# The down products of three MLP groups as seven products per quad of blocks and two token halves

## The chip, the cores and the metric

One core of a Trainium2 chip. The metric is the device time of one execution in microseconds; before the change three runs gave 1750.44, 1750.79 and 1751.02 us.

## The reference, cut to what matters

Two transformer blocks in float32 on x[1, 512, 1024]. The first has differential and forgetting attention with a gated MLP; the second, on the output of the first, has two layers (a short convolution, then latent attention), each with a squared-ReLU MLP. The change concerns the MLP of the last layer alone:

```python
def squared_relu_mlp(h, w_up, w_down):
    return jnp.square(jax.nn.relu(h @ w_up)) @ w_down      # 1024 -> 4096 -> 1024

    h = modulate(rmsnorm_2(x, norm_g[l, 2]), sh_f, sc_f)
    y = squared_relu_mlp(h, mlp_up_w[l], mlp_down_w[l])
    x = x + g_f[:, None, :] * rmsnorm_2(y, norm_g[l, 3])
```

## The kernel before, in words

Activations lie transposed: 128 features in the partitions, 512 tokens in the free dimension, so x, y and h are 8 tiles of 128x512. All weights come as one stream of blocks of 128x1024 (`wstream`); a block holds, for 128 output features, the 8 pieces of 128x128 for the 8 input tiles. Every operand of a matmul is split in a high part (rounded to the type fp32r) and a low part (the rest), and a product is three matmuls: high by high, high weight by low activation, low weight by high activation (L2032 to L2034). A block of 8 pieces is 24 matmuls of 512 columns into one PSUM bank.

A weight block passes four stations, each with 4 slots. SP loads it into `w_raw` (L739) as soon as the low part of the block four before is made (`wlo_done`); ScalarE makes the high part (`split_hi`, L815), three blocks ahead of TensorE (`AHEAD`); VectorE makes the low part (`split_lo`, L1206); TensorE uses both. A bank is reused four blocks later, when VectorE has evacuated it (`bank_free`).

`make_plan` (L76) writes the order of the stages, and each engine goes through this list on its own, in program order, with semaphores between them. At the start of each stage ScalarE and VectorE drain their pipelines (L1086, L1879). The last MLP has four groups of 1024 hidden features: an up stage (`relu2`, 8 blocks) writes 8 hidden tiles, a down stage (`acc`, 8 blocks) adds their products to y. Of each up block, ScalarE takes the ReLU out of PSUM (L893), VectorE multiplies it by the bank (L1433), ScalarE makes the high part (L895) and VectorE the low part (L1316, `rhs_ready`). In a down stage VectorE makes a low part, waits for the product and adds the bank to y (L1397 the first time, L1399 after). The last group ends with a tail of three blocks in two halves of 256 tokens (L2351 to L2353).

VectorE also works off 112 rows of a modulation product (`weighted`, L1217), whose rows POOL loads (L762); eight of them lie in the first down stage of the last MLP, one per block. An up stage without such rows is a loop on VectorE.

In the down stage VectorE's step, here without the cases of other stages, is:

```python
split_lo(t.n + AHEAD, (t.n0 + AHEAD) % SPLIT)
dve.wait_ge(out_done, t.o + 1)
dve.tensor_tensor(dst, dst, bank, ALU.add).then_inc(bank_free, 1)
```

## Time and profile before

| | |
|---|---|
| median of the runs | 1750.79 us (1750.44 to 1751.02) |
| span of the profiled execution | 1748.6 us, 2.2 us under the median of the runs |
| TensorE matmuls | 1730.2 us, 99% of the span, 8136 of them |
| VectorE, ScalarE, POOL | 1100.9, 628.6, 99.1 us |
| granted TensorE clock, mean | 0.999 of 2.4 GHz |
| weights | 283 blocks of 512 KB, 3.6 us each from issue to landing |

Busy time of matmuls overlaps: one of 512 columns is shown with 0.39 us, but the next starts 0.23 us later, so pace is read from starts. The idle time of an engine is shown ahead of the instruction that ended it, with what released it. The span runs from the first to the last instruction. The page gives no time of the profiled execution beyond this span.

### The profile page before, as it was taken

To read this page: it belongs to the slowest core of one execution; us is meant where nothing else is said; L and a number is where in the kernel's file an instruction comes from. 1 tells how busy PE (TensorE), PEld (TensorE's weight loads), DVE (VectorE), ACT (ScalarE), POOL (GpSimd) and SP (SyncE) were. 2 spreads that over 40 slices of the span, in tenths; PEclk is the share of its full clock that TensorE was granted. 3 is DMA by queue.
4 is the path that set the end of the run, shared out by engine and by line. 5 is a ranking of instruction groups with operands and counts; after the bars stand their busy time and mean duration, and the time that the engine had idled before them with its cause. 6 is when DMAs were issued, how large, how long until landed. Compare 5 with 4: busy or idle time off the path is not lost. (4 is left out here: it accounts for less than half of the span.)

```text
span 1748.6 us, 22691 instructions
## 1 busy us (share of the span) xinstructions
PE 1730.2 (99%) x8136; PEld 1404.5 (80%) x8136; DVE 1100.9 (63%) x1641; ACT 628.6 (36%) x991; POOL 99.1 (6%) x158
## 2 busy tenths in 40 slices
PE   9999999999999999999999999999999999999998
PEld 8777777888888888888888888887767888888887
DVE  7866555655555576878656565688775965434356
ACT  5236444322222353243423241444444442323241
POOL 0000000000000000100100101002000100000001
PEclk9999999999999999999999999999999999999999
DMA  7321112454444434652255555531411234323231
GB/s 248 110 96 37 49 49 76 153 169 147 147 162 153 136 102 135 219 184 94 84 180 191 194 192 193 180 109 54 121 61 49 85 101 164 104 88 107 86 97 48
DMA packets 62095, 216.63 MB, mean 124 GB/s; under 512 B 7232, under 2 KB 9408, under 8 KB 61824
## 3 DMA queue, kind: packets, MB, share of 16 engines
q1 hardware_dynamic: 45072, 154.95, 26.2%
q0 software_dynamic: 16656, 60.04, 11.1%
q8 instruction: 49, 0.80, 0.2%
q10 hardware_dynamic: 288, 0.59, 0.1%
q14 instruction: 30, 0.25, 0.0%
HBM read 212.67 MB, written 2.10 MB: 123 GB/s over the span
## 5 line engine op out<-in xcount | busy, mean ns | idle before, releaser
L815 ACT ACTIVATE w_hi<-w_raw 128x1024 fp32r<-128x1024 f32 x283 | 297.7, 1053 | 378.3 <-PE psum L2034 338.9
L1206 DVE TENSOR_TENSOR w_lo<-w_raw,w_hi 128x1024 fp32r<-128x1024 f32 x283 | 346.1, 1223 | 118.6 <-ACT w_hi L815 109.7
L2032 PE MATMUL psum<-h_hi,w_hi 128*128 128x512 f32 x1056 | 411.7, 390 | 0.0
L2033 PE MATMUL psum<-h_lo,w_hi 128*128 128x512 f32 x1056 | 410.8, 389 | 0.0
L2034 PE MATMUL psum<-h_hi,w_lo 128*128 128x512 f32 x1056 | 410.8, 389 | 0.0
L2032 PE MATMUL psum<-hid_hi,w_hi 128*128 128x512 f32 x728 | 283.2, 389 | 0.0
L2033 PE MATMUL psum<-hid_lo,w_hi 128*128 128x512 f32 x728 | 283.2, 389 | 0.0
L2034 PE MATMUL psum<-hid_hi,w_lo 128*128 128x512 f32 x728 | 283.2, 389 | 0.0
L2032 PEld LDWEIGHTS psum<-h_hi,w_hi 128*128 128x128 f32 x1056 | 198.2, 188 | 41.7 <-issue 0.5
L2033 PEld LDWEIGHTS psum<-h_lo,w_hi 128*128 128x128 f32 x1056 | 198.2, 188 | 41.6 <-issue 0.5
L2034 PEld LDWEIGHTS psum<-h_hi,w_lo 128*128 128x128 f32 x1056 | 198.2, 188 | 41.4
L2034 PEld LDWEIGHTS psum<-hid_hi,w_lo 128*128 128x128 f32 x728 | 136.6, 188 | 28.5
L2033 PEld LDWEIGHTS psum<-hid_lo,w_hi 128*128 128x128 f32 x728 | 136.6, 188 | 28.4
L2032 PEld LDWEIGHTS psum<-hid_hi,w_hi 128*128 128x128 f32 x728 | 136.6, 188 | 28.2
L1217 DVE SCALAR_TENSOR_TENSOR ada_raw<-ada_raw,c_row 128x1024 f32<-128x1024 f32 x112 | 136.4, 1219 | 0.9 <-DMA ada_raw<-in_ada 0.8
L762 POOL DMA_DIRECT2D ada_raw<-in_ada x112 | 59.3, 530 | 1134.0 <-DVE ada_raw L1217 1092.1
L1316 DVE TENSOR_TENSOR hid_lo<-scratch,hid_hi 128x512 fp32r<-128x512 f32 (+1 forms) x94 | 65.1, 693 | 75.7 <-ACT hid_hi L895 52.7
L1433 DVE TENSOR_TENSOR scratch<-scratch,psum 128x512 f32<-128x512 f32 x64 | 43.9, 686 | 90.0 <-ACT scratch L893 90.0
L893 ACT ACTIVATE scratch<-psum 128x512 f32<-128x512 f32 x64 | 38.1, 596 | 141.5 <-PE psum L2034 134.6
L1399 DVE TENSOR_TENSOR y<-y,psum 128x512 f32<-128x512 f32 (+1 forms) x37 | 25.4, 688 | 89.7 <-PE psum L2034 89.6
L2007 PE MATMUL psum<-h_hi,w_hi 128*128 128x512 f32 x152 | 61.3, 403 | 1.6 <-ACT h_hi L1113 1.0
L895 ACT ACTIVATE hid_hi<-scratch 128x512 f32 (+1 forms) x64 | 40.5, 633 | 60.2 <-DVE scratch L1433 60.2
(346 smaller groups left out, 2003.6 us busy)
## 6 DMA issues: line engine op xcount, KB each, us to landing
w_raw<-in_wstream SPq DMA_DIRECT2D x283, 512.0 KB, 3.6
ada_raw<-in_ada POOLq DMA_DIRECT2D x112, 512.0 KB, 3.8
x<-in_xT SPq DMA_DIRECT2D x8, 256.0 KB, 5.7
outT<-x SPq DMA_DIRECT2D x16, 128.0 KB, 1.8
con<-in_consts SPq DMA_DIRECT2D x1, 1032.0 KB, 10.0
w_raw<-in_wstream SPq DMA_DIRECT2D x4, 256.0 KB, 4.9
con<-in_rope ACTq DMA_DIRECT2D x1, 576.0 KB, 6.5
c_row<-in_crow POOLq DMA_DIRECT2D x1, 512.0 KB, 4.1
```

Of the source, the lines that this page charges most:

```text
L762: pool.dma_start(ada_raw[:, half, :], ada[v]).then_inc(ada_loaded[half], 16)
L815: act.activation(w_hi[:, slot, :], w_raw[:, slot, :], ACT.Copy).then_inc(whi_done, 1)
L893: act.activation(scratch[:, 2 + t.j % 2, :], bank, ACT.Relu).then_inc(gate_done, 1)
L895: act.activation(tile_of(hi_out, t.b), scratch[:, 8, :], ACT.Copy).then_inc(hi_done, 1)
L1206: dve.tensor_tensor(w_lo[:, slot, :], w_raw[:, slot, :], w_hi[:, slot, :].bitcast(F32), ALU.subtract).then_inc(wlo_done, 1)
L1217: dve.scalar_tensor_tensor(out=row, in0=row, scalar=1.0, in1=c_row[:, :], op0=ALU.mult, op1=ALU.mult, accum_out=ada_sum[:, u:u + 1]).then_ ...
L1316: dve.tensor_tensor(tile_of(lo_out, d), scratch[:, 8, :], tile_of(hi_out, d).bitcast(F32), ALU.subtract).then_inc(rhs_ready, 1)
L1433: dve.tensor_tensor(val, scratch[:, 2 + t.j % 2, :], bank, ALU.mult).then_inc(bank_free, 1)
L2007: pe.matmul(bank, w_hi[:, slot, w], hi[:, ra + k, :], start=k == 0, stop=False)
L2032: pe.matmul(bank, w_hi[:, slot, w], hi[:, ra + k, :], start=k == 0, stop=False)
L2033: pe.matmul(bank, w_hi[:, slot, w], lo[:, ra + k, :], start=False, stop=False)
L2034: mm = pe.matmul(bank, w_lo[:, slot, w], hi[:, ra + k, :], start=False, stop=k == nk - 1)
```

## The change

In the first three groups of the last MLP the down stage (8 blocks) becomes a stage `quads` of two quads. A quad is four blocks: two by two pieces of the weight, where the output side is split in two pairs of 128 features and the input side in even and odd hidden tiles. The tokens are split in two halves of 256, so the activations are two by two pieces as well. The product of these two-by-two matrices is made from seven products instead of eight, by sums of weights, sums of activations and sums of results. Each of the seven, named A12, A11, A, B, C, D, A22 in this order, has 2 output blocks x 4 input pieces x 3 = 24 matmuls of 256 columns and fills one bank.

- Weights. A = a21 + a22 is made by transfers: SP loads a21 into the slot, then POOL issues a transfer of a22 that adds to it. B = A + A11 and C = B + A12 are made by VectorE in slots of `w_raw`, D = A11 + a21 by VectorE in a buffer `w_diff`, into which SP loads a21 once more. Blocks of a quad: four before, six transfers now.
- Activations. In the up stages of these groups the hidden tiles are taken in pairs. After each second tile VectorE makes four sums of 256 columns (`pair_sums`), ScalarE copies three high parts (the odd tile, the even tile, the three sums as one of 768 columns) and VectorE makes the three low parts.
- Results. B accumulates in the bank of A11, C in that of A, D in that of B; each waits for the evacuation before it. VectorE evacuates each product into y, D into two places.
- VectorE's order in step t of `quads`: the weight sums due up to four products ahead, the low part of product t + 3, then the evacuation of product t. In the first step B and C are due, in the second D.
- The first quad of a stage does the first three input pieces of A12 and A11, then the last one of both.
- The eight modulation rows go from the first down stage to the up stage of the last group. SP's loop over blocks is written out, the ring of POOL's descriptors is set to 8192 bytes, and the tail's root takes another bank.

```diff
+    def quads(hid, first):
+        add("quads", dict(n=QUADS * QUAD, o=QUADS * QUAD, quad=QUADS), r0=hid, first=first)
+    def mlp(h, up, down, *names, ends=0, paired=(), **last):
         for g in range(4):
             hid = counts["rhs"]
-            gemm("relu2", 8, "h", h, kouter=AHEAD if g == 0 else 0, presplit=1 if g == 0 else 0, rows=up[g])
+            gemm("relu2", 8, "h", h, kouter=AHEAD if g == 0 else 0, presplit=1 if g == 0 else 0, rows=up[g],
+                 paired=g in paired)
             if g == 3:
                 take(*names)
+            if g in paired:
+                quads(hid, g == 0)
+                continue
             gemm("acc", 8 - (ends if g == 3 else 0), "hid", hid, dst="y", first=g == 0, sq=g == 3, rows=down[g],
                  go_on=ends > 0, **(last if g == 3 else {}))
...
-    hid = mlp(h, (0, 0, 0, 0), (8, 0, 0, 0), "r_f1", ends=ENDS)
+    hid = mlp(h, (0, 0, 0, 8), (0, 0, 0, 0), "r_f1", ends=ENDS, paired=(0, 1, 2))
...
+                a12, a11, a21, a22 = range(at_block, at_block + 4)
+                for u, src in ((U_A12, (a12,)), (U_A11, (a11,)), (U_A, (a21, a22)), (U_B, ()), (U_C, ()), (U_D, (a11, a21)),
+                               (U_A22, (a22,))):
...
+        def quad_bank(s, u):
+            return psum[:, (s["at"]["o"] + QUADS * QUAD + (0, 2, 1, 2, 1, 2, 3)[u]) % BANKS, :]
+        def quad_operand(u, k):
+            if u == U_A11 or u == U_A:
+                col = slice(0, HALF) if u == U_A11 else slice(HALF, S)
+                return hid_hi[:, 2 * k, col], hid_lo[:, 2 * k, col]
+            if u == U_A12 or u == U_C:
+                col = slice(0, HALF) if u == U_A12 else slice(HALF, S)
+                return hid_hi[:, 2 * k + 1, col], hid_lo[:, 2 * k + 1, col]
+            g = {U_B: 1, U_D: 0, U_A22: 2}[u]
+            return sums_hi[:, g, k, :], sums_lo[:, g, k, :]
...
+            for n in range(RAW, NB):
+                u, src, quad = SOURCE[n]
+                slot = n % RAW
+                if u in (U_B, U_C, U_D):
+                    continue
                 sp.wait_ge(wlo_done, n + 1 - RAW)
-                src = wstream[n] if isinstance(n, int) else wstream[bass.ds(n, 1)].rearrange("a p m -> (a p) m")
-                sp.dma_start(w_raw[:, slot, :], src).then_inc(raw_loaded[slot], 16)
-
-            with sp.Fori(1, NB // RAW) as i:
-                for j in range(RAW):
-                    load(RAW * i + j, j)
-            for n in range(NB // RAW * RAW, NB):
-                load(n, n % RAW)
+                made = 2 * sum(SOURCE[m][0] == U_C for m in range(n)) - (1 if SOURCE[n - 1][0] == U_C else 0)
+                if made and (u == U_A22 or any(SOURCE[m][0] is not None for m in range(n - RAW, n))):
+                    sp.wait_ge(sum_made, 2 * quad + 1 if u == U_A22 else 2 * quad if u is not None else made)
+                if u == U_A:
+                    sp.dma_start(w_raw[:, slot, :], wstream[src[0]]).then_inc(sum_begun, 16)
+                    if quad:
+                        sp.wait_ge(wlo_done, last_of(U_D, n) + 1)
+                    sp.dma_start(w_diff[:, :], wstream[SOURCE[n - U_A + U_D][1][1]]).then_inc(diff_loaded, 16)
+                else:
+                    sp.dma_start(w_raw[:, slot, :], wstream[src[0]]).then_inc(raw_loaded[slot], 16)
...
+                if s["kind"] == "quads":
+                    for q in range(QUADS):
+                        n, k = s["at"]["n"] + q * QUAD, s["at"]["quad"] + q
+                        slot = (n + U_A) % RAW
+                        pool.wait_ge(sum_begun, 16 * (k + 1))
+                        pool.dma_start(w_raw[:, slot, :], wstream[SOURCE[n + U_A][1][1]], accum_op=ALU.add)\
+                            .then_inc(sum_loaded, 16)
+                        pool.wait_ge(sum_loaded, 16 * (k + 1))
+                        pool.sem_inc(raw_loaded[slot], 16)
...
+                        if s.get("paired"):
+                            if t.b % 2:
+                                i, p = t.b // 2, at_["pair"] + t.b // 2
+                                act.wait_ge(bank_free, BANKS + t.o + 1)
+                                act.activation(hid_hi[:, t.b, :], scratch[:, 1, :], ACT.Copy).then_inc(hi_done, 1)
+                                act.wait_ge(pair_step, 4 * p + 2)
+                                act.activation(hid_hi[:, t.b - 1, :], scratch[:, 0, :], ACT.Copy).then_inc(hi_done, 1)
+                                act.wait_ge(pair_step, 4 * p + 4)
+                                act.activation(sums_hi[:, :, i, :], pair_sum[:, :, :], ACT.Copy).then_inc(hi_done, 1)
...
+                for t in range(QUADS * QUAD):
+                    n = n0 + t + AHEAD
+                    u, _, quad = SOURCE[n]
+                    if u == U_D:
+                        act.wait_ge(out_done, o0 + t)
+                        act.wait_ge(diff_made, quad + 1)
+                        act.activation(w_hi[:, n % SPLIT, :], w_diff[:, :], ACT.Copy).then_inc(whi_done, 1)
+                    else:
+                        split_hi(n // RAW + 1, n % SPLIT, o0 + t)
...
+            def pair_sums(p):
+                b11, b12, b21, b22 = (scratch[:, i, half_of(h)] for i in range(2) for h in range(2))
+                g3, g2, g4 = (pair_sum[:, i, :] for i in range(3))
+                dve.tensor_tensor(g3, b22, b12, ALU.subtract).then_inc(pair_step, 1)
+                dve.wait_ge(pair_step, 4 * p + 1)
+                dve.tensor_tensor(b12, b11, b12, ALU.subtract).then_inc(pair_step, 1)
+                dve.wait_ge(pair_step, 4 * p + 2)
+                dve.scalar_tensor_tensor(out=g2, in0=b22, scalar=-1.0, in1=b12, op0=ALU.mult, op1=ALU.subtract).then_inc(pair_step, 1)
+                dve.wait_ge(pair_step, 4 * p + 3)
+                dve.scalar_tensor_tensor(out=g4, in0=g2, scalar=-1.0, in1=b21, op0=ALU.mult, op1=ALU.subtract).then_inc(pair_step, 1)
+            def quads(s):
+                n0, o0 = s["at"]["n"], s["at"]["o"]
+                def weight_sum(n):
+                    u, _, quad = SOURCE[n]
+                    if u == U_D:
+                        m = n - U_D + U_A11
+                        dve.wait_ge(diff_loaded, 16 * (quad + 1))
+                        dve.wait_ge(raw_loaded[m % RAW], 16 * (m // RAW + 1))
+                        dve.tensor_tensor(w_diff[:, :], w_raw[:, m % RAW, :], w_diff[:, :], ALU.add).then_inc(diff_made, 1)
+                        return
+                    slot, before = n % RAW, (n - 1) % RAW
+                    other = (n - 2) % RAW if u == U_B else slot
+                    for m in (n - 1, n - 2 if u == U_B else n - 4):
+                        dve.wait_ge(raw_loaded[m % RAW], 16 * (m // RAW + 1))
+                    dve.wait_ge(wlo_done, n - RAW + 1)
+                    dve.tensor_tensor(w_raw[:, slot, :], w_raw[:, before, :], w_raw[:, other, :], ALU.add)\
+                       .then_inc(raw_loaded[slot], 16)
+                    dve.wait_ge(raw_loaded[slot], 16 * (n // RAW + 1))
+                    dve.sem_inc(sum_made, 1)
+                def of_tiles(Q, i, h):
+                    return y[:, 4 * Q + i:4 * Q + i + 3:2, half_of(h)]
+                sums = [n0 + Q * QUAD + u for Q in range(QUADS) for u in (U_B, U_C, U_D)]
+                for t in range(QUADS * QUAD):
+                    Q, u = divmod(t, QUAD)
+                    n, o = n0 + t, o0 + t
+                    while sums and sums[0] <= n + AHEAD + 1:
+                        weight_sum(sums.pop(0))
+                    m = n + AHEAD
+                    if SOURCE[m][0] == U_D:
+                        dve.wait_ge(whi_done, m + 1)
+                        dve.tensor_tensor(w_lo[:, m % SPLIT, :], w_diff[:, :], w_hi[:, m % SPLIT, :].bitcast(F32),
+                                          ALU.subtract).then_inc(wlo_done, 1)
+                        dve.sem_inc(raw_loaded[m % RAW], 16)
+                    else:
+                        split_lo(m, m % SPLIT)
+                    bank = quad_bank(s, u).rearrange("p (a n) -> p a n", a=2)
+                    dve.wait_ge(out_done, o + 1)
+                    dve.wait_ge(bank_free, BANKS + o)
+                    into = {U_A12: (0, 0), U_A11: (0, 0), U_A: (1, 1), U_B: (0, 1), U_C: (0, 1), U_D: (1, 0), U_A22: (1, 0)}[u]
+                    dst = of_tiles(Q, *into)
+                    fresh = s["first"] and u in (U_A12, U_A, U_B, U_D)
+                    minus = u in (U_A, U_D, U_A22)
+                    if u == U_D:
+                        also = of_tiles(Q, 1, 1)
+                        dve.tensor_tensor(also, also, bank, ALU.subtract)
+                    if fresh and minus:
+                        z = dve.tensor_scalar(dst, bank, -1.0, None, ALU.mult)
+                    elif fresh:
+                        z = dve.tensor_copy(dst, bank)
+                    else:
+                        z = dve.tensor_tensor(dst, dst, bank, ALU.subtract if minus else ALU.add)
+                    z.then_inc(bank_free, 1)
...
+                        i, odd = divmod(t.b, 2)
+                        dve.wait_ge(gate_done, at_["gate"] + t.b + 1)
+                        dve.wait_ge(rhs_ready, at_["rhs"] + 3 * i)
+                        dve.tensor_tensor(scratch[:, odd, :], scratch[:, 2 + t.j % 2, :], bank, ALU.mult).then_inc(bank_free, 1)
+                        if odd:
+                            dve.wait_ge(bank_free, BANKS + t.o + 1)
+                            pair_sums(at_["pair"] + i)
+                            for part, (lo, val, hi) in enumerate((
+                                    (hid_lo[:, t.b, :], scratch[:, 1, :], hid_hi[:, t.b, :]),
+                                    (hid_lo[:, t.b - 1, :], scratch[:, 0, :], hid_hi[:, t.b - 1, :]),
+                                    (sums_lo[:, :, i, :], pair_sum[:, :, :], sums_hi[:, :, i, :]))):
+                                dve.wait_ge(hi_done, at_["hi"] + 3 * i + part + 1)
+                                dve.tensor_tensor(lo, val, hi.bitcast(F32), ALU.subtract).then_inc(rhs_ready, 1)
...
+                def product(Q, u, ks):
+                    n = n0 + Q * QUAD + u
+                    bank = quad_bank(s, u)
+                    adds = u in (U_B, U_C, U_D)
+                    for part in range(2):
+                        out = bank[:, half_of(part)]
+                        for k in ks:
+                            hi, lo = quad_operand(u, k)
+                            w = slice((4 * part + k) * P, (4 * part + k + 1) * P)
+                            pe.matmul(out, w_hi[:, n % SPLIT, w], hi, start=not adds and part == 0 and k == 0, stop=False,
+                                      skip_group_check=True)
+                            pe.matmul(out, w_hi[:, n % SPLIT, w], lo, start=False, stop=False, skip_group_check=True)
+                            mm = pe.matmul(out, w_lo[:, n % SPLIT, w], hi, start=False, stop=True, skip_group_check=True)
+                    return mm
+                for Q in range(QUADS):
+                    n, o = n0 + Q * QUAD, o0 + Q * QUAD
+                    free = (o - 2, o - 4, o - 1, o + U_A11, o + U_A, o + U_B, o - 3) if Q == 0 else \
+                        (o - QUAD + U_A12, o - QUAD + U_D, o - QUAD + U_C, o + U_A11, o + U_A, o + U_B, o - QUAD + U_A22)
+                    if Q == 0:
+                        for ks in (range(3), range(3, 4)):
+                            for u in (U_A12, U_A11):
+                                if ks[0] == 0:
+                                    pe.wait_ge(wlo_done, n + u + 1)
+                                    pe.wait_ge(bank_free, BANKS + free[u] + 1)
+                                pe.wait_ge(rhs_ready, s["r0"] + 3 * ks[-1] + (1 if u == U_A12 else 2))
+                                mm = product(Q, u, ks)
+                                if ks[0] == 3:
+                                    mm.then_inc(out_done, 1)
+                        pe.wait_ge(rhs_ready, s["r0"] + 3 * 4)
+                    for u in range(2 if Q == 0 else 0, QUAD):
+                        pe.wait_ge(wlo_done, n + u + 1)
+                        pe.wait_ge(bank_free, BANKS + free[u] + 1)
+                        product(Q, u, range(4)).then_inc(out_done, 1)
...
+    nc = bacc.Bacc("TRN2", target_bir_lowering=False, num_devices=1, dynamic_dma_scratch_size=8192)
```

## Rows read from the trace of the kernel before

**Rows 1.** The page, part 1: busy us, share of the span, instructions of each engine.
```profile
PE 1730.2 (99%) x8136; PEld 1404.5 (80%) x8136; DVE 1100.9 (63%) x1641; ACT 628.6 (36%) x991; POOL 99.1 (6%) x158
```
**Rows 2.** TensorE's waits, longest first: waiter, releaser, us in total, times, longest.
```profile
PE psum L1995 <- DVE eps L1196: 1.6, 1, 1.6
```
**Rows 3.** Windows, first and third down stage: length, busy us, granted clock, DMA share, GB/s.
```profile
1432.46:1475.98 43.52, 43.52 (x193) 36.04 (x192) 23.41 (x31) 9.72 (x10) 3.23 (x6) 1.00 0.49 173
...
1606.54:1650.06 43.52, 43.52 (x193) 36.04 (x192) 16.01 (x17) 9.73 (x10) 0.00 (x0) 1.00 0.36 107
```
**Rows 4.** Timeline of TensorE, tail's second half: start, us, line, operands, count.
```profile
1731.96 0.29 PE L2353 MATMUL psum<-hid_hi,w_lo 128*128 128x256 f32 x1
...
1738.80 0.28 PE L2353 MATMUL psum<-hid_hi,w_lo 128*128 128x256 f32 x1
```
**Rows 5.** Timeline of TensorE, first matmul of the first down stage.
```profile
1432.46 0.39 PE L2032 MATMUL psum<-hid_hi,w_hi 128*128 128x512 f32 x1
```
**Rows 6.** Timeline of VectorE, first down stage and the up stage behind it.
```profile
1433.29 0.69 DVE L1433 TENSOR_TENSOR scratch<-scratch,psum 128x512 f32<-128x512 f32 x1 [1.88 <-ACT scratch L893]
1434.68 0.69 DVE L1316 TENSOR_TENSOR hid_lo<-scratch,hid_hi 128x512 fp32r<-128x512 f32 x1 [0.70 <-ACT hid_hi L895]
...
1438.10 0.69 DVE L1397 COPY y<-psum 128x512 f32<-128x512 f32 x1 [0.72 <-PE psum L2034]
1438.71 1.22 DVE L1217 SCALAR_TENSOR_TENSOR ada_raw<-ada_raw,c_row 128x1024 f32<-128x1024 f32 x1
...
1439.85 1.22 DVE L1206 TENSOR_TENSOR w_lo<-w_raw,w_hi 128x1024 fp32r<-128x1024 f32 x1
...
1478.34 1.23 DVE L1206 TENSOR_TENSOR w_lo<-w_raw,w_hi 128x1024 fp32r<-128x1024 f32 x1 [0.33 <-DVEq L1879]
1482.42 0.69 DVE L1433 TENSOR_TENSOR scratch<-scratch,psum 128x512 f32<-128x512 f32 x1 [2.85 <-ACT scratch L893]
```
**Rows 7.** Timeline of VectorE in the tail: operations of 256 columns.
```profile
1733.97 0.48 DVE L1610 SCALAR_TENSOR_TENSOR psum<-y,r_f,psum 128x256 f32<-128x256 f32 x1
1734.49 0.42 DVE L1625 TENSOR_TENSOR x<-x,psum 128x256 f32<-128x256 f32 x1
1734.83 0.47 DVE L1610 SCALAR_TENSOR_TENSOR y<-y,r_f,psum 128x256 f32<-128x256 f32 x1
```
**Rows 8.** Groups of ScalarE, 1340 to 1749 us: line, operands, count, busy, mean ns, idle before.
```profile
L815 ACT ACTIVATE w_hi<-w_raw 128x1024 fp32r<-128x1024 f32 x69 | 72.7, 1053 | 115.5 <-PE psum L2034 114.5 <-ACTq L1086 1.0
...
L895 ACT ACTIVATE hid_hi<-scratch 128x512 f32 x24 | 15.2, 633 | 21.0 <-DVE scratch L1433 21.0
```
**Rows 9.** Timeline of TensorE, its last matmuls.
```profile
1740.09 0.70 PE L2337 MATMUL psum<-scratch,mean 128*128 128x256 f32 x2 [0.58 <-ACT scratch L1076]
```
**Rows 10.** Windows behind the last matmul, columns as in rows 3.
```profile
1743.00:1744.00 1.00, 0.00 (x0) 0.00 (x0) 1.00 (x4) 0.00 (x0) 1.00 (x2) 0.84 0.14 48
1744.00:1748.60 4.60, 0.00 (x0) 0.00 (x0) 2.07 (x6) 0.00 (x0) 1.02 (x2) 0.50 0.66 218
```
**Rows 11.** Windows of line L1995 (128x128 matmuls) at the opening: length, busy, clock, DMA.
```profile
1.56:6.30 4.74, 4.74 (x22) 1.00 0.97 249
6.30:6.95 0.65, 0.65 (x8) 1.00 1.03 359
```
**Rows 12.** The page, part 6: transfers, count, KB each, median us to landing.
```profile
w_raw<-in_wstream SPq DMA_DIRECT2D x283, 512.0 KB, 3.6
ada_raw<-in_ada POOLq DMA_DIRECT2D x112, 512.0 KB, 3.8
...
con<-in_consts SPq DMA_DIRECT2D x1, 1032.0 KB, 10.0
```
**Rows 13.** Window of the opening, columns as in rows 3.
```profile
10.00:20.00 10.00, 10.00 (x45) 8.16 (x44) 9.16 (x13) 9.23 (x15) 0.00 (x0) 1.00 1.04 413
```
**Rows 14.** The page, part 5: the loads issued by POOL.
```profile
L762 POOL DMA_DIRECT2D ada_raw<-in_ada x112 | 59.3, 530 | 1134.0 <-DVE ada_raw L1217 1092.1
```

More of the change, by code:

```diff
@@ L52 @@
 ROOT_WARM, NEW_WARM = 3, 7
+QUAD, QUADS = 7, 2
+U_A12, U_A11, U_A, U_B, U_C, U_D, U_A22 = range(QUAD)
 SHIFT = 1
@@ L78, in make_plan @@
     counts = dict(n=0, o=0, gate=0, tap=0, sqv=0, ss=0, val=0, hi=0, rhs=0, xup=0, sqa=0, aux=0, rstd=0,
-                  take=0, gains=4, ada=0, rope=0, xpool=0, vs=0, step=0, shift=0)
+                  take=0, gains=4, ada=0, rope=0, xpool=0, vs=0, step=0, shift=0, pair=0, quad=0)
     plan = []
@@ L103, in gemm @@
         if evac == "relu2":
-            inc.update(gate=nblk, hi=nblk, rhs=nblk)
+            parts = nblk // 2 * 3 if about.get("paired") else nblk
+            inc.update(gate=nblk, hi=parts, rhs=parts, pair=nblk // 2 if about.get("paired") else 0)
         if evac == "conv":
@@ L291, with weight_sources @@
 NB = TOTALS["n"]
+def weight_sources():
+    table, at_block = {}, 0
+    for s, after in zip(PLAN, [p["at"]["n"] for p in PLAN[1:]] + [NB]):
+        n = s["at"]["n"]
+        if s["kind"] == "quads":
[3 more added lines that the diff above has]
+                               (U_A22, (a22,))):
+                    table[n + u] = (u, src, s["at"]["quad"] + q)
+                n += QUAD
+                at_block += 4
+        while n < after:
+            table[n] = (None, (at_block,), None)
+            n += 1
+            at_block += 1
+    return table, at_block
+SOURCE, BLOCKS = weight_sources()
 LAST_GEMM = max(i for i, s in enumerate(PLAN) if s["kind"] == "gemm")
@@ L776, in _ @@
                     done = upto
+                if s["kind"] == "quads":
+                    for q in range(QUADS):
+                        n, k = s["at"]["n"] + q * QUAD, s["at"]["quad"] + q
[5 more added lines that the diff above has]
+                        pool.sem_inc(raw_loaded[slot], 16)
                 if s["kind"] == "renew":
@@ L902, in step @@
                         act.activation(tile_of(hi_out, t.of(3) + s.get("f0", 0)), scratch[:, 8, :], ACT.Copy).then_inc(hi_done, 1)
-                steps(act, s, step, last)
+                if s.get("paired"):
+                    for b in range(s["nblk"]):
+                        step(Step(s, b, b, 0, s["nblk"]))
+                else:
+                    steps(act, s, step, last)
+            def quads(s):
[9 more added lines that the diff above has]
+                        split_hi(n // RAW + 1, n % SPLIT, o0 + t)
             def open_stage(s):
@@ L2493, in tiles, with push_quads @@
         return w.reshape(K // P, P, M // P, P).transpose(2, 1, 0, 3).reshape(M // P, P, K)
+    def push_quads(w):
+        t = tiles(w).reshape(2, 2, 2, P, DT // 2, 2, P)
+        t = t.transpose(0, 2, 5, 3, 1, 4, 6).reshape(2, 4, P, D)
+        blocks.append(t[:, (1, 0, 2, 3)].reshape(8, P, D))
     def push(t, per=1):
@@ L2519, in lay_out, with mlp @@
     push(tiles(f["conv_out_w_2"][0]))
-    def mlp(l):
+    def mlp(l, paired=()):
         for g in range(4):
             push(tiles(f["mlp_up_w_2"][l][:, g * D:(g + 1) * D]))
-            push(tiles(f["mlp_down_w_2"][l][g * D:(g + 1) * D]))
+            down = f["mlp_down_w_2"][l][g * D:(g + 1) * D]
+            push_quads(down) if g in paired else push(tiles(down))
     mlp(0)
```

41 lines of the change are left out of this document (32 added, 9 removed).

## Prediction

> **What bounds the kernel now.** I read the page's busy shares first: TensorE is busy for 1730.2 of 1748.6 us, VectorE for 63% and ScalarE for 36% [rows 1]. Then TensorE's waits: the longest is 1.6 us, and that is the opening [rows 2]. So the time is TensorE's, and only fewer TensorE cycles, or a new hole in its stream, can change it. Third, the stretches of the last MLP: a down group takes 43.52 us with TensorE busy for all of it at full granted clock, while VectorE is busy for 16 to 23 us [rows 3].
>
> Times are worked out against the profiled execution, whose span is 1748.6 us; the median of the runs, 1750.79 us, is 2.2 us more. That remainder lies at start and end, which the change leaves alone, so I add differences to the median.
>
> **TensorE's work.** A down group is 8 blocks of 24 matmuls of 512 columns, one every 0.2267 us (43.52 / 192) [rows 3]. The 256-column form exists in the tail: from 1731.96 to 1738.80 us there are 57 steps, 0.120 us each [rows 4]. Half the columns therefore cost 53% of the time. A quad goes from 4 x 24 x 0.2267 = 21.76 us to 7 x 24 x 0.120 = 20.16 us, a group of two quads from 43.52 to 40.32 us. Gain: 3.20 us a group, 9.6 us in all, where seven eighths of the time would have been 16.3 us.
>
> **VectorE at the handover, the first quad of each group.** Let 0 be the start of a group's first matmul (1432.46 in the trace [rows 5]). Unit prices on VectorE: a 1024-column operation lasts 1.22 us and lets the next start after 1.14; a 512-column one 0.69 and 0.61 [rows 6]. In the tail a 256-column scalar_tensor_tensor lasts 0.48, a tensor_tensor 0.42, and one that needs the result of the one before starts 0.04 after its end [rows 7].
>
> Before, the last square is multiplied on VectorE from 0.83 to 1.52 and its low part is done at 2.91 [rows 6]; TensorE has seven earlier tiles to work on meanwhile, so nothing waits. Now the chain goes on: four dependent operations of pair_sums (2 x 0.46 + 2 x 0.52) from 1.56 to about 3.46. Low parts of two tiles, paced by 0.61, end at about 4.1 and 4.7. The high part of the three sums (768 columns) starts on ScalarE when pair_sums ends; between 0.63 for 512 and 1.05 for 1024 columns [rows 8] I take 0.84, so 4.35. Its low part starts at 4.6 and lasts between 0.69 and 1.22, say 0.96: 5.55. The stage's fence on VectorE costs 0.33 [rows 6]: 5.9.
>
> Then the quads stage, in program order: weight sum B (1.22 + 0.04 for the wait on itself + 0.05 for the semaphore step, 1.3), weight sum C (1.3), low part of B (1.14), evacuation of A12 (0.61), weight sum D (1.14), low part of C (1.14), evacuation of A11 (0.69). Together 7.3: the bank of A11 is free at 13.2, known to TensorE at 13.3.
>
> TensorE meanwhile: the first two products in portions, 36 + 12 matmuls of 0.12, to 5.76 (their waits at 4.1 and 4.7 are just met), product A to 8.64. Product B accumulates into the bank of A11, so it waits for that evacuation: **a hole of 4.65 us in every group**. From there both engines run in step. A quad asks VectorE for ten 1024-column operations and eight of 512, 10 x 1.14 + 8 x 0.61 = 16.3 of 20.16 us, so it keeps up, and so does ScalarE with 7 x 1.05 = 7.4 us.
>
> A group becomes 40.32 + 4.65 = 44.97 us instead of 43.52, 1.45 us more, 4.35 us for three. Bounds of the hole: if every wait and latency on VectorE were free and only its pacing counted (0.83 + 0.61 + 2 x 0.34 + 2 x 0.39 + 2 x 0.61 + 0.87 + 5 x 1.14 + 0.61 + 0.69), A11 would be free at 12.0 and the hole 3.3, hardly more than the gain. If a semaphore step costs 0.2 and the 768-column operations as much as 1024-column ones, it is 5.4, which makes 2.2 us a group. I take 4.65, since nearly each duration in it has a row.
>
> **TensorE's clock after the hole.** After its last matmul, which ends at 1740.79 [rows 9], TensorE stays idle; the granted clock is 0.84 in 1743 to 1744 us, and 0.50, the 1.2 GHz level, from 1744 on [rows 10]. A mean of 0.84 puts the fall at 1743.68, 2.9 us after that end. My hole is idle for 4.5 us (A's last matmul ends at 8.80), so the clock can fall in it. The price: at the opening the first 22 small matmuls take 4.74 us, 0.22 each, and the next 8 take 0.65, 0.08 each [rows 11] (the granted clock stands as 1.00 there, but the pace is that of a lower level). So some 4.7 us of work may pass before the full pace is back, at about half, and one fall costs about 2.4 us. With one delay seen, and a hole only 1.6 us longer, I count one fall in three holes: 2.4 us. Bounds: none (0) and all three (7.1).
>
> **The accumulating transfer.** The trace has none. For the first quad of a group its slot is free four blocks ahead, over 20 us, so any price is hidden. For the second quad, the slot of A follows that of D, whose low part is done at 13.2 + 1.2 = 14.4. The load takes 3.6 us [rows 12]: 18.0. Then the accumulating one. VectorE comes to weight sum B of that quad at 23.4 (after product D's two evacuations), and needs 9.1 us from there to the evacuation of the second A11 at 32.5, which TensorE wants at 33.5. So the transfer, with POOL's waits, is hidden up to about 6.0 us, and each us more costs 1 us per group. From below, a plain 512 KB load by POOL lands in 3.8 us, and adding to what is there can't be quicker; from above, 1032 KB land in 10.0 in the crowded opening [rows 12]. I take 3.8 and a second pass over 512 KB at the 413 GB/s that the opening sustains [rows 13], 1.3: 5.1 us, hidden with under 1 us to spare. The rate is no matter: six transfers a quad are 156 GB/s.
>
> **The rest, at nothing.** The eight modulation rows (1.22 us each [rows 6]) go from the first down group to the last up group, where VectorE idles 2.85 us before a square [rows 6]; without that cover they would cost up to 9.8 us. In the up groups pair_sums and the low part of the sums add 2.9 us per two blocks (10.88 us), in the same idle time. SP's loads are written out instead of looped; its new waits are met by VectorE's weight sums, behind them stand loads alone, and the first that matters is priced above. POOL waits in its quads entries with nothing else due. The smaller descriptor area could only delay POOL's modulation loads, ahead of which POOL sat waiting for VectorE 1092.1 us in all [rows 14]. The tail's other bank changes no count.
>
> Sum: 1750.8 - 9.6 + 13.95 + 2.4 = **1757.5 us**.
>
> **Rivals.**
> - *The clock falls in every hole.* The idle time that the fall took at the end, 2.9 us, is shorter than each hole, and then each costs its 2.4 us: 1750.8 - 9.6 + 13.95 + 7.1 = 1762.2. Against: one fall seen, in an end where TensorE had stood for 0.58 us just before [rows 9], and no such hole in mid-kernel. 15%. The Trainium skill ("TensorE: Matmul & The Clock Gate", section "Why this matters for your kernels") speaks for it: it advises to leave no idle gaps between bursts of matmuls, because one is enough to bring the half clock back.
> - *The accumulating transfer is late.* Its time decides from 6.0 us on. At 8 us each second quad has a hole of 2 us more: 1757.5 + 6 = 1763.5; at 10 us, 1769.5. For it: the 10.0 of the large load, and that the load to w_diff is issued at the same moment. Against: the 3.8 of POOL's plain loads beside SP's. 18%.
> - *The hole is near its floor and the clock holds.* With holes of 3.3 to 4.3 us and no fall the sum is 1750.8 - 9.6 + 9.9 to 12.9 = 1751.1 to 1754.1. For it: the full clock in the rest of the stretch [rows 3]. Against: it needs VectorE's waits to vanish. 17%.
> - *The other side: the hole does not outgrow the gain.* VectorE gets to the evacuation of A11 early. It decides where that evacuation ends before 8.64 + 3.20 = 11.84, 1.4 us earlier than I find. With one weight sum and one low part less ahead of it, it ends at 10.8, the holes are 2.2 us, and the time is 1750.8 - 9.6 + 6.6 = 1747.8; with no hole it is 1741.2. For it: VectorE is idle for 20 to 27 of 43.5 us in a down group [rows 3]. Against: that idle time lies behind the handover, and the pacing alone gives 12.0. 8%.
> - *The forecast*: holes of about 4.65 us, a fall in some, the transfer hidden: 42%, by itself 1754.5 to 1760.
>
> Differences under 0.2% (3.5 us) cannot be told from none. Slower: 42 + 15 + 18 = 75%; within: 17%; faster: 8%. The range leaves out the faster case and the far end of the late transfer: 1752 to 1768.
>
> **What would show it.** In the profile after: 256-column matmuls of the quads in steps of 0.12 us; an idle stretch of TensorE of 4 to 5 us in each of the three groups, ahead of product B of the first quad, released by VectorE's evacuation; before that release two weight sums, a low part, an evacuation, a weight sum and a low part on VectorE without a break; and a dip of the granted clock where a hole was. A second hole, in the second quad and with POOL's transfer behind it, would show the late transfer. If no hole stands at product B, or the steps are over 0.13 us, the prediction is wrong in its main step.

## The result, and the profile after

| | before | after |
|---|---|---|
| median of the runs, us | 1750.9 (4 runs, 1750.44 to 1751.82) | 1762.8 (4 runs, 1761.47 to 1764.21) |
| profiled execution: span, us | 1748.6 | 1759.6 |
| TensorE busy, us | 1730.2 | 1726.7 |
| VectorE busy, us | 1100.9 | 1183.6 |

The ratio of the times is 1.0067 [1.0053, 1.0081]: slower, by 0.7%. The predicted 1757.5 us is 5.3 us too low, inside the range of 1752 to 1768.

The page's first part, after, answers to [rows 1]: TensorE works 3.5 us less and the program lasts 11.0 us more.
```profile
PE 1726.7 (98%) x8568; PEld 1422.6 (81%) x8568; DVE 1183.6 (67%) x1761; ACT 657.3 (37%) x1021; POOL 104.2 (6%) x164
```
Windows of the three changed down groups, after, columns as in [rows 3] (stretch, length, busy us of PE, PEld, DVE, ACT and POOL, granted clock, DMA share, GB/s):
```profile
1432.81:1479.82 47.01, 42.25 (x337) 41.90 (x336) 37.59 (x43) 17.43 (x18) 0.88 (x1) 0.96 0.50 144
1523.37:1570.95 47.58, 42.87 (x338) 42.69 (x337) 37.66 (x43) 17.43 (x18) 0.86 (x1) 0.93 0.51 144
1614.49:1661.04 46.55, 41.83 (x338) 41.65 (x336) 37.58 (x43) 17.43 (x18) 0.86 (x1) 0.96 0.51 147
sum 141.14, PE 126.95 PEld 126.24 DVE 112.84 ACT 52.29 POOL 2.59; mean PE 42.32 PEld 42.08 DVE 37.61 ACT 17.43 POOL 0.86
```
This is the whole account. Three groups took 3 x 43.52 = 130.56 us before and take 141.14 now: 10.6 of the span's 11.0 us. In them TensorE is idle for 141.14 - 126.95 = 14.2 us, and busy for 6.0 us more than the 3 x 40.32 that the shorter products need at full pace. So: 130.56 - 9.6 + 14.2 + 6.0 = 141.2. Not all of the 6.0 us is the clock: by the starts, the matmuls of the 6 us behind the three stops take 1.56, 2.39 and 1.35 us more than at 0.12 each, 5.3 in sum; most of the rest is the last matmul before each stop, which shows its whole 0.28 us because no next one overlaps it.

Where it is idle: TensorE's timeline in the first group, after (start, us, line, operands, count, in brackets the idle time before it and what ended it). Product A ends in steps of 0.12 us; product B starts 4.72 us later, released by VectorE's evacuation at L1481, and soon goes on in steps of 0.21 us, until 0.12 is back at 1450.04.
```profile
1441.20 0.28 PE L2294 MATMUL psum<-hid_lo,w_hi 128*128 128x256 f32 x1
1441.32 0.28 PE L2295 MATMUL psum<-hid_hi,w_lo 128*128 128x256 f32 x1
1446.32 0.36 PE L2292 MATMUL psum<-sums_hi,w_hi 128*128 128x256 f32 x1 [4.72 <-DVE y L1481]
1446.51 0.33 PE L2294 MATMUL psum<-sums_lo,w_hi 128*128 128x256 f32 x1
...
1449.42 0.41 PE L2292 MATMUL psum<-sums_hi,w_hi 128*128 128x256 f32 x1
1449.63 0.41 PE L2294 MATMUL psum<-sums_lo,w_hi 128*128 128x256 f32 x1
...
1450.04 0.28 PE L2292 MATMUL psum<-sums_hi,w_hi 128*128 128x256 f32 x1
1450.16 0.29 PE L2294 MATMUL psum<-sums_lo,w_hi 128*128 128x256 f32 x1
```
The same stop stands in the other two groups (4.71 and 4.72 us). Windows of the three stops and of what follows each, after, columns as above: the granted clock falls to 0.5, the 1.2 GHz level, at each of them, and comes back to 1.00 after 3 to 5 us of work. Over the stops themselves it is 1.00, 0.84 and 0.95 in the mean: at the first stop it fell only when work had begun again, at the others inside the stop.
```profile
1441.60:1446.32 4.72, 0.00 (x1) 0.03 (x1) 4.72 (x6) 2.67 (x3) 0.00 (x0) 1.00 0.54 199
1446.32:1450.00 3.68, 3.68 (x18) 3.68 (x19) 2.72 (x3) 0.22 (x1) 0.00 (x0) 0.54 0.70 188
1450.00:1452.00 2.00, 2.00 (x19) 2.00 (x18) 0.69 (x1) 1.04 (x1) 0.00 (x0) 1.00 0.91 287
1532.16:1536.87 4.71, 0.00 (x0) 0.03 (x1) 4.71 (x6) 2.66 (x3) 0.00 (x0) 0.84 0.62 202
1536.87:1542.00 5.13, 5.13 (x24) 5.13 (x25) 2.72 (x3) 0.22 (x1) 0.00 (x0) 0.50 0.69 241
1542.00:1544.00 2.00, 2.00 (x18) 2.00 (x18) 1.24 (x2) 1.06 (x1) 0.00 (x0) 0.96 0.43 168
1623.28:1628.00 4.72, 0.01 (x1) 0.03 (x1) 4.72 (x6) 2.67 (x3) 0.00 (x0) 0.95 0.58 193
1628.00:1631.00 3.00, 3.00 (x14) 3.00 (x15) 2.73 (x3) 0.22 (x1) 0.00 (x0) 0.51 0.73 191
1631.00:1633.00 2.00, 2.00 (x19) 2.00 (x19) 0.56 (x1) 0.56 (x1) 0.00 (x0) 1.00 0.90 281
```
What VectorE does meanwhile: its timeline from the last square of the up stage (answers to the first lines of [rows 6]) to the evacuation that TensorE waits for. From the first of these lines on, no bracket names TensorE; the chain is VectorE's own, without a break of over 0.33 us.
```profile
1433.64 0.69 DVE L1618 TENSOR_TENSOR scratch<-scratch,psum 128x512 f32<-128x512 f32 x1 [3.26 <-ACT scratch L977]
1434.36 0.43 DVE L1418 TENSOR_TENSOR pair_sum<-scratch 128x256 f32<-128x256 f32 x1
...
1436.08 1.29 DVE L1627 TENSOR_TENSOR hid_lo<-scratch,hid_hi 128x512 fp32r<-128x512 f32 x2
1437.29 0.95 DVE L1627 TENSOR_TENSOR sums_lo<-pair_sum,sums_hi 128x768 fp32r<-128x768 f32 x1
1438.57 1.23 DVE L1443 TENSOR_TENSOR w_raw<-w_raw 128x1024 f32<-128x1024 f32 x1 [0.33 <-DVEq L2077]
1440.11 1.23 DVE L1443 TENSOR_TENSOR w_raw<-w_raw 128x1024 f32<-128x1024 f32 x1 [0.31 <-DVE w_raw L1443]
1441.48 1.23 DVE L1318 TENSOR_TENSOR w_lo<-w_raw,w_hi 128x1024 fp32r<-128x1024 f32 x1
1442.62 0.68 DVE L1479 COPY y<-psum 128x512 f32<-128x512 f32 x1
1443.22 1.22 DVE L1436 TENSOR_TENSOR w_diff<-w_raw,w_diff 128x1024 f32<-128x1024 f32 x1
1444.35 1.22 DVE L1318 TENSOR_TENSOR w_lo<-w_raw,w_hi 128x1024 fp32r<-128x1024 f32 x1
1445.49 0.68 DVE L1481 TENSOR_TENSOR y<-y,psum 128x512 f32<-128x512 f32 x1
```
The accumulating transfer shows no stop of its own after (the longest step before product B of a second quad is 0.32 us in the first group). Its chain in the first group: D's low part ends at 1447.31 (14.5 us after the group's start), SP loads A's first term for the second quad (issued at 1447.33), POOL can issue the accumulating transfer only at 1453.00, and VectorE's weight sum B of that quad starts at 1458.93, after an idle time that no compute engine ended. Timelines of SP, POOL and VectorE, after:
```profile
1447.33 0.33 SPq L815 DMA_DIRECT2D w_raw<-in_wstream  x1
1447.71 0.42 SPq L818 DMA_DIRECT2D w_diff<-in_wstream  x1
...
1453.00 0.88 POOL L857 DMA_DIRECT2D w_raw<-in_wstream  x1 [31.36 <-DMA w_raw<-in_wstream]
...
1458.93 1.23 DVE L1443 TENSOR_TENSOR w_raw<-w_raw 128x1024 f32<-128x1024 f32 x1 [0.92 <-issue]
```
So load and accumulation take 5.7 + 5.9 us here, 6.3 + 5.5 and 5.3 + 5.8 in the other groups, where the prediction had 3.6 + 5.1. Experiments e6 to e8 ask why that cost nothing.

### The profile page after: what moved, and what is told of

It is laid out like the page before. It is cut to its first block and busy times, and to the rows that moved or that the text cites. A ratio compares the mean times of both kernels' runs of the same rounds, so it can differ in the third digit from the quotient of the medians.

```text
span 1759.6 us, 22662 instructions
## 1 busy us (share of the span) xinstructions
PE 1726.7 (98%) x8568; PEld 1422.6 (81%) x8568; DVE 1183.6 (67%) x1761; ACT 657.3 (37%) x1021; POOL 104.2 (6%) x164
## 5 line engine op out<-in xcount | busy, mean ns | idle before, releaser
L2234 PE MATMUL psum<-h_hi,w_lo 128*128 128x512 f32 x1056 | 410.8, 389 | 0.0
L2232 PE MATMUL psum<-hid_hi,w_hi 128*128 128x512 f32 x536 | 208.5, 389 | 0.0
L2233 PE MATMUL psum<-hid_lo,w_hi 128*128 128x512 f32 x536 | 208.5, 389 | 0.0
L2234 PE MATMUL psum<-hid_hi,w_lo 128*128 128x512 f32 x536 | 208.5, 389 | 0.0
L2234 PEld LDWEIGHTS psum<-hid_hi,w_lo 128*128 128x128 f32 x536 | 100.6, 188 | 21.0
L2233 PEld LDWEIGHTS psum<-hid_lo,w_hi 128*128 128x128 f32 x536 | 100.6, 188 | 20.9
L2232 PEld LDWEIGHTS psum<-hid_hi,w_hi 128*128 128x128 f32 x536 | 100.6, 188 | 20.8
L1500 DVE TENSOR_TENSOR hid_lo<-scratch,hid_hi 128x512 fp32r<-128x512 f32 x70 | 48.5, 692 | 54.2 <-ACT hid_hi L989 31.2
L2208 PE MATMUL psum<-h_hi,w_lo 128*128 128x512 f32 x152 | 59.4, 391 | 0.0
L1631 DVE TENSOR_TENSOR scratch<-scratch,psum 128x512 f32<-128x512 f32 x40 | 27.5, 687 | 46.6 <-ACT scratch L977 46.6
L2292 PE MATMUL psum<-sums_hi,w_hi 128*128 128x256 f32 x144 | 43.5, 302 | 14.2 <-DVE y L1481 14.2
```

The costliest lines, as they stand in the source:

```text
L1500: dve.tensor_tensor(tile_of(lo_out, d), scratch[:, 8, :], tile_of(hi_out, d).bitcast(F32), ALU.subtract).then_inc(rhs_ready, 1)
L2208: pe.matmul(bank, w_lo[:, slot, w], hi[:, ra + k, :], start=False, stop=False)
L2232: pe.matmul(bank, w_hi[:, slot, w], hi[:, ra + k, :], start=k == 0, stop=False)
L2233: pe.matmul(bank, w_hi[:, slot, w], lo[:, ra + k, :], start=False, stop=False)
L2234: mm = pe.matmul(bank, w_lo[:, slot, w], hi[:, ra + k, :], start=False, stop=k == nk - 1)
L2292: pe.matmul(out, w_hi[:, n % SPLIT, w], hi, start=not adds and part == 0 and k == 0, stop=False, skip_group_check=True)
```

## The experiments

The theory: the stop is VectorE's chain at the handover; the half clock behind it is a price on top; the transfer hides. The rivals: the chain is not what product B waits for, or the clock's price is no price.

**e1_warm_hole.** Keep TensorE at work in the stop, so that the clock can't fall:
```diff
                     for u in range(2 if Q == 0 else 0, QUAD):
+                        if Q == 0 and u == U_B:
+                            keep_warm(34)
                         pe.wait_ge(wlo_done, n + u + 1)
```


> The changed kernel with 34 small matmuls (128x128, into a bank that nobody reads) ahead of product B of each stage's first quad, about 4.2 us of work in a hole of 4.9 us. VectorE's chain is untouched, so product B still starts as late. Theory (hole plus clock): the granted clock holds, the 5.1 us that the three falls cost come back, and the time is 1757 us (1755.5 to 1758.5). Rival (the clock costs nothing of its own, the rest is lost elsewhere, as to the late transfer or to contention): it stays at 1762.8. Rival (the gate falls for another reason than idleness, such as the 256-column form): the dips stay and so does the time.

Measured: 1763.77 us (1763.37 to 1764.07), ratio 1.0076 [1.0062, 1.009]. The clock stayed at full, but I had mis-sized the filler: each of the 34 calls is two matmuls, so it lasts 7.76 us and outlives the stop by some 3 us. TensorE's timeline of e1:
```profile
1440.82 7.76 PE L2195 MATMUL psum<-mean 128*128 128x128 f32 x68
1448.34 0.36 PE L2292 MATMUL psum<-sums_hi,w_hi 128*128 128x256 f32 x1
```
The groups are 47.90 us long, 40.32 + 7.58. This run says nothing of the clock's price; e6 repeats it at the right size. It does answer the rival on the 256-column form: the same matmuls stand here, and with TensorE kept at work the clock did not fall.

**e2_sums_early.** Take the three weight sums of each group's first quad out of the handover, into the up stage's loop, where VectorE waits for squares:
```diff
+                        if s.get("paired"):
+                            for u in {4: (U_D,), 6: (U_B, U_C)}.get(b, ()):
+                                weight_sum(at_["n"] + s["nblk"] + u)
...
-                sums = [n0 + Q * QUAD + u for Q in range(QUADS) for u in (U_B, U_C, U_D)]
+                sums = [n0 + QUAD + u for u in (U_B, U_C, U_D)]
```


> The changed kernel with the three weight sums of each stage's first quad made by VectorE in the up stage (D after its fifth block, B and C after its seventh); the order within the quads stage stays. Theory: 3.7 us of weight sums leave the chain ahead of the evacuation of A11, the hole shrinks from 4.9 to about 0.8 us, too short for the clock to fall, and a group takes 41.3 us: 1750.9 + 0.4 - 6.7 = 1744.6 us (1743 to 1747), faster than before. Rival (the transfers are what costs): the weight sums were not the bound, the time stays above 1757. Rival (VectorE's work in the up stage now delays the hidden tiles): a hole appears at the start of the stage, and the time is 1748 or more.

Measured: 1750.26 us (1748.88 to 1755.25), ratio 1.0003 [0.9994, 1.0012]. The stop before product B of the first quad shrank as expected, in groups 2 and 3 from 5.00 to 0.82 us between starts: the chain is its cause. But 5.7 us of the expected gain are missing, because a stop opened elsewhere: before product B of the *second* quad, 3.02, 1.64 and 2.19 us between starts in the three groups, the first with a fall of the clock. Timelines of POOL, VectorE and TensorE in e2's second group:
```profile
1538.90 0.86 POOL L857 DMA_DIRECT2D w_raw<-in_wstream  x1 [34.46 <-DMA w_raw<-in_wstream]
...
1544.40 1.23 DVE L1440 TENSOR_TENSOR w_raw<-w_raw 128x1024 f32<-128x1024 f32 x1 [2.24 <-issue]
...
1553.71 0.35 PE L2295 MATMUL psum<-sums_hi,w_hi 128*128 128x256 f32 x1 [1.36 <-DVE y L1481]
```
VectorE is now idle for 2.24 us ahead of weight sum B, and starts 5.5 us after POOL's issue, which points to the transfer; e3 tests it. In group 1 the last of the expected rivals, late hidden tiles, came true as well: VectorE, with the early sums ahead of it, starts the last square 2.12 us after the group's start (0.83 in group 2), and TensorE stops for 1.11 us between starts at the first portions and for 0.99 before product B.

**e4_evac_first.** The changed kernel with one reorder: the first two evacuations of a quads stage ahead of its weight sums and low parts.
```diff
+                def low(t):
...
+                def evacuate(t):
...
+                evacuate(0)
+                evacuate(1)
+                for t in range(QUADS * QUAD):
+                    low(t)
+                    if t >= 2:
+                        evacuate(t)
```


> The changed kernel with nothing made earlier, only reordered: at the start of a quads stage VectorE evacuates A12 and A11 before it makes the weight sums. Theory: product B no longer waits for its bank but for its own weights (weight sums B, C and the low part of B lie ahead), the hole is split: 2.5 us before B, 1.2 before C, and about 1.3 in the second quad, as VectorE has no slack left. Each piece is shorter than the 2.9 us after which the clock fell in the idle end, so it holds: 1756.5 us (1754 to 1759). If the clock falls in pieces of 2.5 us too: 1760 or more. Rival (only the evacuation was the cause, the sums are free): no hole, 1742.

Measured: 1762.2 us (1760.55 to 1766.44), ratio 1.0073 [1.0059, 1.0087]. The stop went to 2.73 us between starts, near the 2.5 expected, and product B now waits for its own low part instead of the bank:
```profile
1443.94 0.39 PE L2302 MATMUL psum<-sums_hi,w_hi 128*128 128x256 f32 x1 [2.46 <-DVE w_lo L1318]
...
1468.66 0.55 PE L2302 MATMUL psum<-sums_hi,w_hi 128*128 128x256 f32 x1 [2.82 <-DVE y L1484]
```
What it saved came back twice: the clock fell at these stops as well, as the second expectation (1760 or more) had it, and second-quad stops of 3.10, 1.37 and 2.52 us opened (the second line above). The three groups together are 141.47 us, against 141.14.

**e5_all_early.** e2, e4's reorder, and SP's load of the second quad's A moved ahead (the diff of that move stands under e3).


> Weight sums of the first quad made in the up stage, evacuations of A12 and A11 first, and SP loads the second quad's A as soon as the sums of the first have read the slot, ahead of the three loads that stood before it. Theory: no hole is left in either quad, every group takes 40.3 us at the full clock: 1750.9 + 0.4 - 9.6 = 1741.7 us (1740.5 to 1744). Rival (a second limit in the quads stage, VectorE's share of 16.3 in 20.16 us or the transfer): holes appear elsewhere, and the time is 1746 or more.

Measured: 1741.73 us (1741.28 to 1742.93), ratio 0.9951 [0.9937, 0.9965], against the kernel before: faster than both. Windows of the three groups in e5:
```profile
1432.65:1473.61 40.96, 40.62 (x337) 40.41 (x336) 35.47 (x42) 17.32 (x18) 0.88 (x1) 1.00 0.54 166
1517.16:1557.47 40.31, 40.31 (x337) 40.31 (x336) 34.31 (x41) 17.32 (x18) 0.86 (x1) 1.00 0.56 159
1601.02:1641.33 40.31, 40.31 (x337) 40.31 (x336) 34.33 (x41) 17.32 (x18) 0.86 (x1) 1.00 0.53 160
```
Two groups run at 40.31 us without a stop; the prediction's price for TensorE's work was 40.32. The first has one step of 0.62 us at its first portions.

**e3_transfer_early.** e2 and SP's move alone, to test what the second-quad stops are:
```diff
+                if SOURCE[n][0] == U_A and SOURCE[n][2] % QUADS:
+                    order.remove(n)
+                    order.insert(order.index(n - QUAD + U_A22 - U_A), n)
...
+                if u == U_A and quad % QUADS:
+                    sp.wait_ge(wlo_done, n - QUAD + U_A11 - U_A + 1)
+                    sp.wait_ge(sum_made, 2 * quad - 1)
+                    sp.wait_ge(diff_made, quad)
+                    sp.dma_start(w_raw[:, slot, :], wstream[src[0]]).then_inc(sum_begun, 16)
+                    continue
```


> The three weight sums of each group's first quad made in the stage before, as in e2, and besides SP loads the first term of the second quad's A as soon as the low part of the first quad's A11 is made, instead of behind D's low part. Nothing else moves. Theory (in e2 the second-quad stops of 3.0, 1.6 and 2.2 us are the transfer: sum B of the second quad waits for it, 5.9 us of load and 5.5 us of accumulation after D's low part): these stops and the clock dip in group 1 go, the 0.83 us stop before product B of the first quad stays, groups of about 41.0 us, 1744 us. Rival (the second-quad stops come from VectorE's own backlog, which the early sums only moved): the stops stay, 1750 us.

Measured: 1744.77 us (1743.86 to 1747.12), ratio 0.9968 [0.9956, 0.998]. The second-quad stops are gone from all three groups, the 0.83 us stop stays in groups 2 and 3. So they were the transfer, load and accumulation together, and not VectorE's backlog. Group 1 keeps stops of 1.16 us at its first portions and 1.00 before product B, as in e2.

**e6_warm_20, e7_early_only, e8_warm_early.** If the transfer is that late, why has the changed kernel no stop at it? Either it had time enough there, or the stretch at half clock made TensorE late as well. Two edits, each alone and both together: e1's filler with 20 calls instead of 34, and SP's early load.

> As e1, dummy matmuls of 128 columns on TensorE in the stop before product B of the first quad, but 20 calls (40 matmuls of 0.114 us, 4.56 us) instead of 34 (7.76 us, which was longer than the stop), so that product B starts where it did. Their result is used nowhere. Clock theory (the price of the falls, 1.5 + 2.3 + 1.3 = 5.1 us, is all on the path): groups of 45.2 us, 1757.7 us. Rival (two covers: in the changed kernel the second quad's transfer is ready, and with it the evacuation of the second A11, only 35.3, 35.5 and 34.8 us after the group's start, where a TensorE without clock falls would come at 33.7): the clock holds, but a stop of 1.1 to 1.9 us opens before product B of the second quad in each group, groups of 46.4 to 47.1 us, about 1762 us.

> The changed kernel with one move alone: SP loads the first term of the second quad's A early, as in e3. Both theories: the stop before product B of the first quad stays at 4.7 us and the clock falls in it, so the transfer's lateness stays covered by the half-clock stretch: 1762.4 us, within 1 us of the changed kernel. A third one, that the transfer itself holds VectorE or TensorE up through traffic: 1758 or less.

> e6 and e7 together: the 20 dummy calls in the stop, and the early load for the second quad's A. Clock theory: as e6 alone, 1757.7 us, so no difference between e6 and e8. Two covers: only now both are gone, each group is 40.32 + 4.9 = 45.2 us, 1757.5 us, about 4.5 us less than e6 and 5 us less than e7.

| second-quad load | clock falls in the stop | clock kept up |
|---|---|---|
| late, as in the change | 1762.8 (the changed kernel) | e6: 1759.64 (1758.94 to 1761.26) |
| early | e7: 1762.65 (1760.41 to 1764.04) | e8: 1757.35 (1756.62 to 1757.47) |

The ratios to the kernel before are 1.0054 [1.004, 1.0068] for e6, 1.0066 [1.0053, 1.008] for e7 and 1.0038 [1.0025, 1.0052] for e8. With the falls in place the early load gains nothing; with the clock kept up it gains 2.3 us. With the early load the clock is worth 5.3 us; without it, 3.1 (2.3 by the ratios, since the changed kernel's own runs stand beside others of the kernel before; the intervals of these two ratios overlap). The sums of the three groups in the profiled executions agree in the order: 141.14 us for the changed kernel, and, columns as above, the first group and the sum of e6 and e7:
```profile
1432.23:1478.47 46.24, 45.23 (x377) 44.90 (x376) 37.59 (x43) 17.43 (x18) 0.88 (x1) 1.00 0.50 148
sum 139.92, PE 135.71 PEld 134.70 DVE 112.72 ACT 52.09 POOL 2.59; mean PE 45.24 PEld 44.90 DVE 37.57 ACT 17.36 POOL 0.86
...
1434.49:1481.89 47.40, 42.68 (x338) 42.50 (x336) 37.67 (x43) 17.54 (x18) 0.88 (x1) 0.93 0.48 144
sum 142.05, PE 127.89 PEld 127.37 DVE 112.96 ACT 52.61 POOL 2.59; mean PE 42.63 PEld 42.46 DVE 37.65 ACT 17.54 POOL 0.86
```
With e8's 137.67 (below) the early load gains 2.3 us with the clock kept up and nothing without, and the clock is worth 4.4 us with the early load and 1.2 without. So each of the two delays covers part of the other, as the rival had it. The trace of e6 shows it: the filler ends before the evacuation, product B starts where it did in the group, and a new stop stands before product B of the second quad, 21 us later (0.76 us idle in this group; 1.04, 1.12 and 2.16 us between starts in the three).
```profile
1440.86 4.63 PE L2195 MATMUL psum<-mean 128*128 128x128 f32 x40
1445.74 0.36 PE L2292 MATMUL psum<-sums_hi,w_hi 128*128 128x256 f32 x1 [0.25 <-DVE y L1481]
...
1466.88 0.36 PE L2292 MATMUL psum<-sums_hi,w_hi 128*128 128x256 f32 x1 [0.76 <-DVE y L1481]
```
By the length of the groups the rival came close: 46.24, 46.32 and 47.36 us stand beside its 46.4 to 47.1, where the clock theory had 45.2. Its new stops were 4.5 us in sum (from 35.3, 35.5 and 34.8 against 33.7); beyond one step of 0.12 each they are 4.0. Its time, about 1762, was too high, because it was counted from the changed kernel's median of 1762.8 us, and the execution whose groups it used took 1761.47. In e8, windows of the three groups:
```profile
1432.32:1478.14 45.82, 45.24 (x378) 44.91 (x376) 37.50 (x43) 17.55 (x18) 0.88 (x1) 1.00 0.49 149
1521.68:1567.48 45.80, 45.22 (x377) 44.88 (x376) 37.40 (x43) 17.55 (x18) 0.86 (x1) 1.00 0.51 149
1611.03:1657.08 46.05, 45.23 (x378) 44.89 (x377) 37.40 (x43) 17.55 (x18) 0.86 (x1) 1.00 0.49 149
```
A group is 40.32 plus the filled stop, 4.9, plus 0.6 to 0.9: the early load has a price, a stop of 0.61 to 0.85 us between starts before product D of the first quad. D accumulates in the bank of B; VectorE evacuates B behind the low part of A22, and ScalarE can make A22's high part only when its load has landed (in the first group its 3.98 us of waiting end with a landing at 1449.08). SP issues that load behind the one moved ahead: the three loads that begin at 1439.37 in e6 begin at 1444.48 here. So the time of e8, 1757.35 us, meets the 1757.5 expected by luck: the groups are longer than the 45.2 expected, and with 45.2 the count would have been 1750.1 + 3 x 45.2 - 130.56 = 1755.1.

## Why the time came out as it did, step by step

- **TensorE's gain, 3.20 us a group: right.** Steps of 0.12 us after; 40.31 us a group in e5.
- **VectorE's chain and the hole of 4.65 us: right.** Idle 4.72, 4.71 and 4.72 us. The evacuation of A11 ends at 13.36 us (predicted 13.2). Inside the chain two sizes were off and cancelled: pair_sums ran faster (1.8 us instead of 1.9 to its end, and the chain reached the first weight sum 5.76 us after the start instead of 5.9), and between the two weight sums the wait on the first with its semaphore step costs 0.31 us, not 0.09. That the weight sums are the larger part of it, e2 shows.
- **"I count one fall in three holes": wrong.** This is the failed step. The clock fell at all three stops of 4.7 us. The price of one fall was sized at 2.4 us, from the 4.7 us that the opening needed (the 0.08 us read there for the full pace is too short: the window also counts matmuls begun before it, and in e1 matmuls of this size go at 0.114); by TensorE's steps the three cost 1.56, 2.39 and 1.35 us, 5.3 in sum, and e7 against e8 gives 5.3 by the medians and 4.4 by the groups. The rival "the clock falls in every hole", 1762.2 us at 15%, is what happened. That its number is within 1 us is in part luck: its falls were 1.8 us too dear, and its holes 0.7 us too short (4.65 each, measured 4.88 beyond one step). The one fall in the trace before, 2.9 us after the last matmul [rows 10], was the better witness, and it stood in the text; I gave it too little weight because it came from the kernel's end. The Trainium skill ("TensorE: Matmul & The Clock Gate", section "Why this matters for your kernels") advises to leave no long idle gaps between bursts of matmuls, because they bring the half clock back. The trace agrees for these stops of 4.7 us; across the 0.82 to 0.83 us of e2 and e3 the clock held.
- **The accumulating transfer, "hidden with under 1 us to spare": right in its effect, wrong in its sizes.** The load that begins it took 5.3 to 6.3 us to POOL's issue, with w_diff's load issued beside it, not 3.6, and the accumulation 5.5 to 5.9, not 5.1. Instead of under 1 us to spare it was about 1 to 2 us late for a TensorE at full clock (e6). It cost nothing, or next to it, because the clock's falls had already made TensorE late by as much (e7, e8). A rival named for it ("late") was thus true as a mechanism and invisible in the time.
- **The rest, at nothing: nearly so.** The first changed group starts 0.35 us later than before (1432.81 against 1432.46), 0.35 of the 11.0 us.
- **The other side (faster): not in this kernel,** but its condition, an earlier evacuation of A11, is what e5 brings about.

What stays open: why the half clock lasted some 5 us of work behind the second stop and 3.0 to 3.7 behind the others; and why VectorE comes late to the last square in group 1 alone of e2 and e3 (2.12 and 2.17 us after the group's start), which opens stops of 0.99 to 1.16 us between starts there.

## What to carry to other kernels

When a change hands a shorter job to the bound engine, add up what another engine must do in a row at the handover before the first buffer comes free: here 13.4 us against the 8.6 us of work at hand, three times, undid a gain of 9.6 us, and moving the weight sums to where that engine idles, with the evacuations first and the second quad's load ahead, brought the gain back (e5, 1741.7 us). Price a stop of TensorE with the half clock behind it: every stop of 2.7 to 5.0 us between starts brought one here. And a cover is only as good as the delay that makes it: after removing one stop, look at what was late behind it (e2, e6), and remove both before judging either.

## What had not been expected of the hardware

- The clock also fell at stops of 2.73 us between starts (e4), in each group, and at one of 3.02 (e2), so that cutting a stop by almost half did not spare the fall. It held across single stops of 2.19 us (e2), 2.17 (e6) and 2.52 (e4).
- It also fell without a stop: in the profiled executions of e3 and e7, each the slowest of its runs, the granted clock drops to 0.50 at 94.1 and 94.4 us, far ahead of the changed groups. TensorE had not been idle there; shortly before it had done 20 matmuls of 8 columns in 2.40 us, as every execution does. In the other profiled executions the clock held there, so a comparison of whole spans with these two is off by it, and the text compares groups.
- At the lower level a 256-column matmul is paced at 0.213 us against 0.120 at full clock: 1.78 times, not 2.
- An accumulating 512 KB transfer took 5.5 to 5.9 us from POOL's issue to the sum that waits for it (5.6 to landing, median of six), where POOL's plain loads of that size land in 3.9.
- Two 512 KB loads that SP issued 0.4 us apart both took longer than one: 5.3 to 6.3 us from the issue for w_raw to POOL's own issue behind it, 5.8 to landing for w_diff (median), against a median of 4.0 for SP's w_raw loads. A third, issued 1.7 us earlier, was still on its way; whether the company is the reason was not tested.
